# Linear attention's output in two runs of products, and the state-space decay sums as two one-pass products

## The reference, cut to what matters

```
a = jnp.einsum('bthd,bshd->bhts', qc * jnp.exp(b - b_mid), kc * jnp.exp(b_mid - b))
a = jnp.where(mask, a, 0.0)
o = jnp.einsum('bhts,bshv->bthv', a, vc) + jnp.einsum('bthd,bhdv->bthv', qc * jnp.exp(b), state)
state = jnp.exp(b_last[:, 0])[..., None] * state + jnp.einsum('bshd,bshv->bhdv', kc * jnp.exp(b_last - b), vc)
```

```
cum = jnp.cumsum(dac, axis=1)
seg = cum[:, :, None] - cum[:, None, :]
decay = jnp.exp(jnp.where(mask, seg, -jnp.inf))
```

## Time and profile before

| | |
|---|---|
| median of 3 runs | 1890.28 us (1889.61 to 1892.07) |
| the profiled execution's own time | 1891.88 us |
| its span, first to last instruction | 1890.2 us |
| PE busy | 1852.4 us, 98% |
| DVE busy | 960.4 us, 51% |
| ACT busy | 609.9 us, 32% |
| POOL busy | 131.8 us, 7% |
| mean granted clock of PE | 0.993 |

### The profile page before, as it was taken

One profiled execution on the slowest core, in us unless ns is written; L12 is line 12 of the kernel. 1 busy time (PEld: TensorE's weight loads), 2 busy tenths in 40 slices (PEclk: granted clock), 3 DMA queues, 4 the chain that ended last, 5 costly groups with the idle time before them and its releaser, 6 DMA issues.

```text
span 1890.2 us, 26212 instructions
## 1 busy us (share of the span) xinstructions
PE 1852.4 (98%) x9852; PEld 1514.2 (80%) x9852; DVE 960.4 (51%) x1360; ACT 609.9 (32%) x942; POOL 131.8 (7%) x126
## 2 busy tenths in 40 slices
PE   7999999989999999999999999999999999999997
PEld 5888888867888888788988878887888888888885
DVE  6444443376888888632533335556433544444333
ACT  4222222233333333332233324444222332222221
POOL 3111100032000000000000000000000011111000
PEclk9999999989999999999999999999999999999998
DMA  4232233311222222232212222222222223223331
GB/s 157 94 100 100 90 103 106 101 60 63 78 68 77 67 67 67 68 100 89 85 66 66 69 74 88 89 88 89 92 97 97 92 90 100 95 94 100 100 104 62
DMA packets 47353, 164.92 MB, mean 87 GB/s; under 512 B 5520, under 2 KB 6672, under 8 KB 47296
## 3 DMA queue, kind: packets, MB, share of 16 engines
q1 hardware_dynamic: 43584, 158.10, 25.4%
q10 hardware_dynamic: 3712, 6.03, 1.0%
HBM read 162.01 MB, written 2.10 MB: 87 GB/s over the span
## 4 chain that ended last, share of the span: by engine, by line
PE 75%; issue 20%; DVE 2%; POOL 2%; DMA 0%; ACT 0%; POOLq 0%; SPq 0%; DVEq 0%; ACTq 0%
PE G L521 36%; PE G L572 12%; PE I L521 9%; PE G L537 7%; PE I L884 1%; POOL hid L423 1%; PE I L918 1%; PE I L859 1%; PE I L894 1%; PE I L858 1%; PE I L698 1%; PE I L706 1%; PE I L672 1%; PE G L755 1%; PE I L715 1%
## 5 line engine op out<-in xcount | busy, mean ns | idle before, releaser
L1431 DVE TENSOR_TENSOR WL<-RAW,WH 128x1024 fp32r<-128x1024 f32 x297 | 375.4, 1267 | 304.9 <-ACT WH L1013 297.0
L1013 ACT CAST WH<-RAW 128x1024 fp32r<-128x1024 f32 x297 | 308.8, 1045 | 236.7 <-PE I L521 131.9
L521 PE MATMUL G<-UH,WH 128*128 128x512 f32 x1136 | 287.9, 395 | 0.0
L521 PE MATMUL G<-UL,WH 128*128 128x512 f32 x1136 | 280.7, 389 | 0.0
L521 PE MATMUL G<-UH,WL 128*128 128x512 f32 x1136 | 280.6, 389 | 0.0
L521 PEld LDWEIGHTS G<-UH,WH 128*128 128x128 f32 x1136 | 212.1, 188 | 51.1 <-issue 7.8
L521 PEld LDWEIGHTS G<-UL,WH 128*128 128x128 f32 x1136 | 213.2, 188 | 44.6
L521 PEld LDWEIGHTS G<-UH,WL 128*128 128x128 f32 x1136 | 213.2, 188 | 44.2
L572 PE MATMUL G<-WH,UH 128*128 128x256 f32 x640 | 92.2, 287 | 3.4 <-DVE WL L1431 3.4
L572 PE MATMUL G<-WL,UH 128*128 128x256 f32 x640 | 91.2, 285 | 0.0
L572 PE MATMUL G<-WH,UL 128*128 128x256 f32 x640 | 90.7, 285 | 0.0
(11 more groups left out here) (284 smaller groups left out, 2164.1 us busy)
## 6 DMA issues: line engine op xcount, KB each, us to landing
RAW<-in_slabs SPq DMA_DIRECT2D x297, 512.0 KB, 3.3
h<-in_x SPq DMA_DIRECT2D x4, 512.0 KB, 6.9
bias<-in_rel ACTq DMA_DIRECT2D x16, 128.0 KB, 2.9
out_y<-h ACTq DMA_DIRECT2D x8, 256.0 KB, 2.2
bias<-in_rel ACTq DMA_DIRECT2D x16, 112.0 KB, 2.8
cst<-in_cst SPq DMA_DIRECT2D x1, 168.0 KB, 3.8
ut<-in_wgk SPq DMA_DIRECT2D x3, 32.0 KB, 8.6
```

Source lines behind the costliest of these rows:

```text
L521: ins = mm(dst, W[:, n.slot, (k - k0) * P:(k - k0 + 1) * P], R[:, k, :], start=begin and which == 0 and k == k0, stop=end and which == 2 a ...
L1013: nc.scalar.copy(WH[:, n.slot, :], RAW[:, n.slot, :]).then_inc(split_hi, 1)
L1431: V.tensor_tensor(WL[:, n.slot, :], RAW[:, n.slot, :], WH[:, n.slot, :].bitcast(F32), ALU.subtract).then_inc(split_lo, 1)
```

## The change

Two edits. In `gla_o` the eight query-state products of a head come first, in a row, and then the eight score-value products. The first product of each bank now clears it, and all others add. In the state-space branch da is split once, on POOL, into a rounded part (fp32r) and a remainder, and the masked table is made twice: of the rounded part by DVE (MSH) and of the remainder by POOL (MSL, new function `da_lo`). PE multiplies both with an fp32r copy of the 0/1 matrix. SC and gsc grow from 24 to 32 rows. The tables no longer lie in M, which holds only the exponentials.

```diff
@@ tensor engine
-                pe.wait_ge(sems["da_masked"], last("da_masked", g))
+                pe.wait_ge(sems["da_hi_masked"], last("da_hi_masked", g))
+                pe.wait_ge(sems["da_lo_masked"], last("da_lo_masked", g))
                 pe.wait_ge(sems["ssm_y"], after("ssm_y", g - 1, 0))
-                rhs = M[:].rearrange("p j r t -> p (j r t)")
                 for s in range(2):
-                    ins = mm(I34[:, s * T:(s + 1) * T], after_s[:], rhs[:, s * T:(s + 1) * T], start=True, stop=True)
+                    dst = I34[:, s * T:(s + 1) * T]
+                    mm(dst, after_r[:], MSH[:, s * T:(s + 1) * T], start=True, stop=False)
+                    ins = mm(dst, after_r[:], MSL[:, s * T:(s + 1) * T], start=False, stop=True)
                 inc(ins, "seg_done")
...
                 for c in range(NCH):
                     j, s = c // 2, half(c)
-                    dst = I01[s, j * 256:(j + 1) * 256]
-                    mm(dst, GA[s, j, :], GV[s, j, :], start=True, stop=False)
-                    ins = mm(dst, QT[:, c * CH:(c + 1) * CH], GS[:, c, :], start=False, stop=True)
+                    mm(I01[s, j * 256:(j + 1) * 256], QT[:, c * CH:(c + 1) * CH], GS[:, c, :], start=j % 2 == 0,
+                       stop=False, skip_group_check=True)
+                for c in range(NCH):
+                    j, s = c // 2, half(c)
+                    ins = mm(I01[s, j * 256:(j + 1) * 256], GA[s, j, :], GV[s, j, :], start=False, stop=True,
+                             skip_group_check=True)
                 inc(ins, "gla_o_done")
@@ POOL: constants, once, and each group
+            link(nc.gpsimd.tensor_copy(after_r[:], after_s[:]))
...
+            def da_lo(g):
+
+                pool.wait_ge(sems["group_const"], after("group_const", g))
+                pool.wait_ge(sems["intra_done"], last("intra_done", g - 1))
+                inc(nc.gpsimd.tensor_tensor(MSL[:].rearrange("p (q t) -> p q t", t=CH),
+                                            bc(gsc[:, 28:32, :].rearrange("p j r -> p (j r)"), CH),
+                                            causal[:].unsqueeze(1).to_broadcast([P, TT * HPG, CH]), ALU.mult),
+                    "da_lo_masked")
...
+                da = SC[:, 0:4, :].rearrange("p j h -> p (j h)")
+                link(g.tensor_copy(DAH[:], da))
+                link(g.tensor_copy(SC[:, 24:28, :].rearrange("p j h -> p (j h)"), DAH[:].bitcast(F32)))
+                link(g.tensor_tensor(SC[:, 28:32, :].rearrange("p j h -> p (j h)"), da, DAH[:].bitcast(F32),
+                                     ALU.subtract))
+                assert step[0] == DA_SPLIT, step
...
             with pool.Fori(0, NG) as i:
+                da_lo(i)
                 ssm(i)
@@ DVE: each group, and one wait once
-                da = gsc[:, 0:4, :].rearrange("p j r -> p (j r)")
-                inc(V.tensor_tensor(M[:].rearrange("p j r t -> p (j r) t"), bc(da, CH),
-                                    causal[:].unsqueeze(1).to_broadcast([P, TT * HPG, CH]), ALU.mult), "da_masked")
+                da = gsc[:, 24:28, :].rearrange("p j r -> p (j r)")
+                inc(V.tensor_tensor(MSH[:].rearrange("p (q t) -> p q t", t=CH), bc(da, CH),
+                                    causal[:].unsqueeze(1).to_broadcast([P, TT * HPG, CH]), ALU.mult), "da_hi_masked")
...
                 dt_to_end()
+                dve.wait_ge(dt_pool, DA_SPLIT)
                 group_scalars(0)
```

More of the change, by code:

```diff
@@ L120 @@
     "vector": {
-        "conv_const": 1, "group_const": 1, "group_norm": 1, "da_masked": 1, "xdt_ready": 1, "xte_ready": 1, "cb_masked": 1,
+        "conv_const": 1, "group_const": 1, "group_norm": 1, "da_hi_masked": 1, "xdt_ready": 1, "xte_ready": 1, "cb_masked": 1,
         "m_ready": 1, "conv_done": 4, "ssm_chain": 13, "ssm_y": 4, "ssm_var": 1, "ssm_scaled": 4, "ssm_lo": 2,
@@ L126 @@
     },
-    "gpsimd": {"xd_ready": 1, "ssm_rstd": 1, "gla_rstd": 1},
+    "gpsimd": {"da_lo_masked": 1, "xd_ready": 1, "ssm_rstd": 1, "gla_rstd": 1},
     "tensor": {
@@ L173, in build @@
         rstd4 = sb("rstd4", [P, TT])
-        SC = sb("SC", [P, 24, HS])
+        SC = sb("SC", [P, 32, HS])
         gconv = sb("gconv", [P, 20])
         ggrp = sb("ggrp", [P, 6])
-        gsc = sb("gsc", [P, 24, HPG])
+        gsc = sb("gsc", [P, 32, HPG])
         minus_a = sb("minus_a", [P, HS])
@@ L184, in build @@
         rms = sb("rms", [P, T], F32, early)
+        early.close()
+        early = ExitStack()
+        sb("first_gate", [P, T], F32, early)
+        MSH = sb("MSH", [P, 2 * T], F32R, early)
         early.close()
@@ L219, in build @@
         BK = sb("BK", [P, TT, P], F32, w)
+        prep = ExitStack()
+        MSL = sb("MSL", [P, 2 * T], F32R, prep)
+        prep.close()
         M = sb("M", [P, TT, HPG, CH], F32, w)
@@ L226, in build @@
         ss4 = sb("ss4", [P, TT], F32, w)
+        after_r = sb("after_r", [P, P], F32R, w)
+        DAH = sb("DAH", [P, TT * HS], F32R, w)
         w.close()
@@ L2001, in _ @@
                                        ALU.mult, ALU.mult).then_inc(out_ready, 1)
-N_CONSTS = 11
+N_CONSTS = 12
 DT_ABS, DA_READY = 2, 22
+DA_SPLIT = DA_READY + 3
 POOL_SQUARES = 4
```

## The result

The changed kernel takes 1856.76 us (median of 4 runs, 1856.05 to 1858.99), the kernel before 1889.94 beside it (4 runs, 1889.45 to 1892.07). The ratio is 0.9824, 95% interval 0.9807 to 0.9841: 33.2 us faster, 1.8%, where 18.6 were forecast. The sign was right, the size was not.

What follows compares the result with a forecast made beforehand. The prediction took PE, busy for 98% of the span, as the bound. Its terms, -21.6 us for linear attention and +3.05 for the state-space part, gave -18.6, so 1871.7 us against the median of 1890.28; range 1865 to 1880 (78%).

Steps and rivals of the forecast that it cites:

- Linear attention's output: In `gla_o`, products grouped by shape take 3.8 us a head instead of 9.19; four heads, -21.6 us.
- a record alone takes 0.205: In `gla_o`, one 256-column fp32 matmul record not run beside another takes 0.205 us, from the decay sums.
- a seam of 0.16: In `gla_o`, the extra time where matmuls of two shapes alternate: 0.16 of a pair's 0.57 us.
- Rival B: In `gla_o`, score-value products don't run side by side: -15.4 us there, 1877.9 us in all; 13%.
- Rival D: In `gla_o`, neither shape runs side by side, only seams go: 6.9 us a call, 1884.1 us in all; 5%.
- What POOL's table costs: State-space groups: POOL's `da_lo` takes 1.91 us and delays DVE; the state-space part sums to +3.05 us.
- push 1.8: State-space groups: POOL's `da_lo` sets DVE's row of work back by 1.8 us through contention.
- C: State-space groups: POOL's product takes 2.54 us, push 2.47, so 1876.2 us in all; 10%.
- Rival A: State-space groups: no contention in the end, groups 0 to 6 win 0.75 us each; 1863.4 us in all; 15%.
- E: State-space loop hangs on POOL's long product, making the kernel slower; the push must exceed 5.0 us; 2%.
- The whole split: State-space part: group 0 -0.75, groups 1 to 6 +2.7, group 7 +1.1; sum +3.05 us.
- Costs at nothing: POOL's three operations ahead of the loop, about 0.5 us each, and the constant's copy at the start cost nothing.

Runs made afterwards that it cites:

- the shift alone: Kernel before plus an unused tensor of 1152 bytes per partition behind gsc, nothing else: 1876.51 us, ratio 0.9931.
- the second pair of kernels: Kernel before with new `gla_o` order and 1152 unused bytes behind gsc, no split, against the changed kernel: 1854.15 us, ratio 0.9817 to the kernel before.
- the pad of 256 bytes: Kernel before with 256 unused bytes per partition behind gsc: 1891.32 us, one run.

## Why the prediction was right and wrong

- **"Linear attention's output", -21.6: right.** 3.8 us a call forecast, 3.76 measured; -21.8 in the trace, -20.7 as a median alone. The steps under it hold too: "a record alone takes 0.205" (0.216 measured, same half in a row), and a seam of 0.16 (0.14 measured). The price of the new runs came from L706, which has the same 1.88. The mechanism was right, and not only the number.
- **Rival B fell.** The score-value products, in different rows and one bank, take the same 1.88 as the query-state ones, start in pairs as these do, and take 2.78 when their halves don't alternate. "TensorEngine Tiling (Array Packing)" of the Trainium skill, section "Gotcha 1: PSUM Pressure", says that different row tiles can't use one bank at the same time; these runs don't agree with it. Rival D falls with the same rows: records of both halves start in pairs, and a call takes 3.76 and not 6.9.
- **"What POOL's table costs": the mechanism right, the sizes somewhat off.** Forecast: push 1.8, +0.45 a round, waits for XTE in seven groups 4 to 6 us beyond 1.4. Measured: push 1.70, +0.33 a round, waits 4.6 in all, 3.2 beyond 1.4, so under the range of 4 to 6. POOL's own time is 1.8, not C's 2.54. Rival A fell: the engines don't share. E stayed far off: the push of 1.70 is a third of the 5.0 that it needs. The whole split is +1.1 by medians (1.3 to 2.6 in the second pair of kernels), where +3.05 was forecast.
- **The step that failed is "Costs at nothing".** It counted the instructions that the change adds, put the larger buffers at nothing without a reason, and so held every matmul of the other stages at its old duration. SC and gsc became longer, and with that the operands of the FFN's down products, both merges and the output product moved by 1152 bytes, from 128 off the weights' address mod 256 to the same. The term is about -13 us (-13.0 in the trace, -12.6 with the shift alone, 12.6 back with 128 bytes moved). With it the sum is -31.6 against -33.2 measured; most of what is left is the split, +1.1 instead of +3.05. The rows for it stood in the profile before. From its page:

```profile
L521 PE MATMUL G<-UL,WH 128*128 128x512 f32 x1136 | 280.7, 389 | 0.0
...
L521 PE MATMUL I<-HH,WH 128*128 128x512 f32 x352 | 89.9, 395 | 0.0
```

The shape and the line are the same, and the means differ by 6 ns. I read both as the price of a matmul and didn't ask why they differ. A mean can mislead here: UH with WH, the first block behind other work, has 395 too, but its median is 389 and its pitch 227.
- **The rest is chance of one execution.** The norm's gain of 3 us is in the profile of the order alone too, which up to linear attention is the same program as before, at the same addresses; the shift alone and the pad of 256 bytes don't have it. So neither edit makes it, and the medians add up without them. It is PE's time at 1.2 GHz at the one place where it costs, and that differs between executions; I don't count it as the change's.

What stays open is what the chip does at addresses that aren't equal mod 256. The runs show the rule and not its cause, and no run tests whether the loading of the weights and the reading of the operand get in each other's way. Distances of every multiple of 32 bytes up to 224 cost 5 to 7 ns; finer ones weren't tried. Why the 256-column products don't follow the rule is open too.

## What to carry to other kernels

If the same instruction on the same shape has two mean durations in a profile, find out what sets it before the change is costed: here 6 to 7 ns a matmul made 13 us, over half of what the larger edit gives, and any edit that changes an allocation's size moves it. Where 512-column fp32r products bound the kernel, place moving operands and weights at addresses that are equal mod 512 (one operand of one run speaks for 256 being enough). Before work is handed from a busy engine to an idle one, compare its price on the busy one with the push that the idle one gives through shared ports: on DVE MSL cost 1.14, on POOL 1.70.

## What the runs showed of the hardware that I had not expected

- A 512-column fp32r product's pitch depends on the operand's address against the weights': 226.7 ns if equal mod 256, 231 to 234 otherwise, over about 2000 of the kernel's matmuls (and over all of UH's and UL's when the weights were moved). Products of 256 columns didn't change.
- Eight fp32 products with 64 output partitions and 256 columns take 1.88 us with alternating halves: records start in pairs, a pair every 0.216 us, also where the two halves have different rows and one PSUM bank. Within one half they start singly, every 0.216. A change between the two shapes costs 0.14.
- POOL's operation gets the ports between two back-to-back operations of DVE: it came 0.12 us after the first, stood until its end, and then held the second up by 1.70.
